# A split-float32 transformer kernel: order of its tensors in the partition

## What is computed

```
m = rms_norm(mem, mem_norm_g)
for layer in (0, 1):
    h = h + mixer(rms_norm(h, mix_norm_g[layer]))
    h = h + memory_cross_attention(rms_norm(h, xa_norm_g[layer]), m, wq, wkv, wo)
    h = h + (gelu(conv3(g) + b) * u) @ w_down,   [u, g] = rms_norm(h) @ w_up
u = rms_norm(h); proj = u @ w_in                  # 9232 columns, second block
h = h + (sigmoid(gate_r) * y_ret + sigmoid(gate_d) * y_dn) @ w_o
h = h + (silu(a) * b) @ w_down,   [a, b] = conv3(rms_norm(h) @ w_up) + b
out = rms_norm(h, g_final)
```

## Time and profile before

| | |
|---|---|
| median of 3 runs | 2487.08 us |
| the profiled execution's own time | 2488.18 us |
| its span, first to last instruction | 2486.4 us |
| TensorE matmuls busy | 2392.3 us, 96% of the span, 10,934 matmuls |
| TensorE weight loads busy | 1926.0 us |
| VectorE, ScalarE, GpSimd busy | 993.0, 865.9, 969.4 us |
| mean granted TensorE clock | 0.99 of full speed |
| read from memory | 213.9 MB, 88 GB/s |

### The profile page before, as it was taken

How to read it: one execution, slowest core, us unless ns; L and a number is a source line. 1 busy time by engine, 2 the same in 40 slices (tenths; PEclk the granted TensorE clock), 3 DMA queues, 4 the chain that set the end, 5 groups by cost and what they waited for, 6 DMA issues and landing times.

```text
span 2486.4 us, 25675 instructions
## 1 busy us (share of the span) xinstructions
PE 2392.3 (96%) x10934; PEld 1926.0 (77%) x10934; DVE 993.0 (40%) x1210; ACT 865.9 (35%) x1048; POOL 969.4 (39%) x389
## 2 busy tenths in 40 slices
PE   8989999999999999999999999988997999999997
PEld 6738878888887887888887768877876888888885
DVE  3053024442244203444226340568458433566601
ACT  4244434322322433433344372351352243322221
POOL 4504713544444561444344314330140144455541
PEclk9999999999999999999999999999999999999998
DMA  7203412333333441323334303420130023333331
GB/s 213 89 0 96 150 43 93 97 99 93 93 97 90 127 128 50 94 93 100 95 98 127 85 26 103 116 77 18 44 93 18 26 93 127 93 100 95 94 95 66
DMA packets 148561, 219.81 MB, mean 88 GB/s; under 512 B 18640, under 2 KB 75216, under 8 KB 148064
## 3 DMA queue, kind: packets, MB, share of 16 engines
q1 hardware_dynamic: 147328, 213.95, 28.5%
q10 hardware_dynamic: 1120, 4.23, 0.5%
HBM read 213.92 MB, written 4.23 MB: 88 GB/s over the span
## 4 chain that ended last, share of the span: by engine, by line
PE 92%; DVE 5%; ACT 2%; issue 1%; DMA 0%; POOL 0%; SPq 0%; ACTq 0%; DVEq 0%
PE ps L916 76%; PE ps L1062 2%; PE ps L1059 2%; PE ps L1280 1%; PE ps L1075 1%; PE ps L1098 1%; PE ps L988 1%; DVE MT L1830 1%; PE ps L1269 1%; PE ps L1168 1%; PE ps L1181 1%; PE ps L1004 1%; PE ps L1221 1%; DVE MM L1834 0%; PE ps L939 0%
## 5 line engine op out<-in xcount | busy, mean ns | idle before, releaser
L474 POOL TENSOR_TENSOR w_lo<-w_raw,w_hi 128x1024 fp32r<-128x1024 f32 x379 | 957.8, 2539 | 1475.8 <-ACT w_hi L511 1475.7
L916 PE MATMUL ps<-XH,w_hi 128*128 128x512 f32 x1792 | 703.0, 392 | 12.7 <-DVE XL L1408 11.9
L511 ACT ACTIVATE w_hi<-w_raw 128x1024 fp32r<-128x1024 f32 x379 | 395.0, 1055 | 887.2 <-DMA w_raw<-ffn_w_up 124.7
L916 PE MATMUL ps<-XH,w_lo 128*128 128x512 f32 x1792 | 698.1, 390 | 0.0
L916 PE MATMUL ps<-XL,w_hi 128*128 128x512 f32 x1792 | 698.1, 390 | 0.0
L916 PE MATMUL ps<-HID,w_hi 128*128 128x512 f32 x1760 | 554.5, 396 | 4.0 <-DVE TY L1613 2.4
L916 PEld LDWEIGHTS ps<-XH,w_hi 128*128 128x128 f32 x1792 | 336.9, 188 | 85.6 <-issue 14.2
L916 PEld LDWEIGHTS ps<-HID,w_hi 128*128 128x128 f32 x1760 | 330.1, 188 | 87.1 <-issue 3.4
L916 PEld LDWEIGHTS ps<-XL,w_hi 128*128 128x128 f32 x1792 | 337.0, 188 | 72.0 <-issue 2.4
L916 PEld LDWEIGHTS ps<-XH,w_lo 128*128 128x128 f32 x1792 | 336.9, 188 | 70.2
L916 PE MATMUL ps<-HID,w_lo 128*128 128x512 f32 x880 | 347.7, 395 | 0.0
(11 more groups left out here) (310 smaller groups left out, 2356.8 us busy)
## 6 DMA issues: line engine op xcount, KB each, us to landing
w_raw<-w_in SPq DMA_DIRECT2D x72, 512.0 KB, 3.7
w_raw<-ffn_w_up SPq DMA_DIRECT2D x128, 256.0 KB, 2.9
w_raw<-w_up SPq DMA_DIRECT2D x88, 256.0 KB, 3.1
w_raw<-xa_wkv SPq DMA_DIRECT2D x32, 512.0 KB, 3.6
w_raw<-ffn_w_down SPq DMA_DIRECT2D x32, 512.0 KB, 3.6
w_raw<-w_in_c SPq DMA_DIRECT2D x24, 512.0 KB, 3.7
w_raw<-w_down SPq DMA_DIRECT2D x22, 512.0 KB, 3.6
w_raw<-w_in_ab SPq DMA_DIRECT2D x16, 512.0 KB, 5.1
```

Of the source, the lines that this page charges most:

```text
L474: nc.gpsimd.tensor_tensor(w_lo[:, s, :, :], w_raw[:, s, :, :], w_hi[:, s, :, :].bitcast(F32), ALU.subtract).then_inc(lo_done, 1)
L511: nc.scalar.activation(w_hi[:, s, :, :], w_raw[:, s, :, :], ACT.Copy).then_inc(hi_done, 1)
L916: mm = nc.tensor.matmul(ps[:, bank + m, :], a, b, start=start and j == 0 and n == 0, stop=stop and j == 1 and n == 2)
```

## The change

The definitions of XH and XL now come first, then the arena with its base a0, then H, the weight rings and the small tensors in their old order. No instruction, size, wait or loop is changed.

```
--- before.py
+++ after.py
@@ -94,9 +94,11 @@
             return ctx.enter_context(nc.semaphore(name))
 
 
-        H = sb("H", [P, KT, T])
         XH = sb("XH", [P, KT, T], F32R)
         XL = sb("XL", [P, KT, T], F32R)
+        a0 = (nc.sbuf_base + 63) // 64 * 64
+        arena = sb("arena", [P, (BIG_SLOTS * T * 4 + TAIL + 64) // 4])
+        H = sb("H", [P, KT, T])
         w_raw = sb("w_raw", [P, RING, 2, UC])
         w_lo = nc.alloc_sbuf_tensor_at("w_lo", [P, RING, 2, UC], F32R, offset=nc.sbuf_base - RING * 2 * UC * 4)
         w_hi = sb("w_hi", [P, RING, 2, UC], F32R)
@@ -110,8 +112,6 @@
         cst = sb("cst", [P, N_CONST, P])
         eps_c = sb("eps_c", [P, 2])
         sm = sb("sm", [P, 128])
-        a0 = (nc.sbuf_base + 63) // 64 * 64
-        arena = sb("arena", [P, (BIG_SLOTS * T * 4 + TAIL + 64) // 4])
         ps = ctx.enter_context(nc.psum_tensor("ps", [P, 8, T], F32))
 
         def at(name, kb, shape, dt=F32):
```

## The result

The changed kernel takes **2522.97 us** (median of 4 runs, 2522.11 to 2525.83); the kernel before, beside it, 2486.71 us (4 runs, 2486.05 to 2490.66). The ratio is 1.0131, 95% interval 1.0119 to 1.0143: slower by 1.3%. The prediction was 2525. The profiled execution took 2522.11 us, against 2488.2 before.

A forecast was written before the change was run, and what follows sets the result against it. It took the kernel to be bound by a stream of TensorE matmuls, number times start-to-start pace. Terms 36.0 + 0 + 1.9 + 0.4 + 0 = +38.3 us on 2487.1 gave 2525 us; range 2471 to 2529.

The forecast's parts named there:

- The main term: XH and XL streaming past loaded weights: 5,400 matmuls go from 226.7 to 233.3 ns, +36.0 us.
- line 1062, a small case: Weights streaming low, MH or ML loaded high: 229.0 and 233.3 ns; taken as the model for XH; itself +0.4 us.
- the 288: Matmuls streaming weights with XH or XL loaded: expected to go to HID's 233.3 ns, +1.9 us.
- the gain that looked due to it: HID streaming, 2,640 matmuls, moved to low addresses: could win 17.6 us at 226.7 ns; taken as 0.
- only the streamed operand's place counts: Rival: HID, now low, speeds up by 17.6 us, XH stays; 2472 to 2474 us, chance 0.22.
- The trace can't tell these two properties apart; each is a place.: Operand lying below or above 92,000 bytes, and start at or 64 past a multiple of 128, treated together; no size.
- Above 233.3 ... none exists either: Rival: split products slower than 233.3 ns, needing high places on both sides, absent after the change; beyond 2529, chance 0.03.
- It becomes what HID is now: high streamed, low loaded: Reason given for matmuls streaming weights past XH or XL to slow to 233.3 ns: +1.9 us.
- Line 1059, "I take 0": 384 matmuls of 256 columns, at 114.5 and 116.4 ns: no change, bounds -0.4 and +0.4 us.
- "Nothing is absorbed": Slower TensorE stretches every stage; its idle time stays the same waits in the same places, so the sum shows fully.
- The faster rival: HID gains from streaming low, XH keeps its pace: 2472 us, or 2474 with HID's upper third above 92,000; chance 0.22.
- The rule of the Trainium skill: Rival for all TensorE matmuls: independent read ports, so addresses change nothing; 2487 us, no effect given chance 0.05.

The follow-up runs named there:

- e8: Kernel before with the weight rings 160 bytes further up and HID starting at 192 modulo 256; 2526.31 us (one run).
- e10: Kernel before with XL alone moved to 192 modulo 256, weights and HID starting alike with XH; 2499.22 us (one run).
- e1: Kernel before with the arena's base rounded up to 128 bytes, so HID, MH and ML lie 64 bytes higher; 2471.82 us, ratio 0.992.
- e2: Changed kernel with the arena 64 bytes longer, so all operands start at multiples of 128; 2518.85 us, ratio to the kernel before 1.0115.

## Why the prediction was right

**The main term.** 5,400 matmuls from 226.7 to 233.3, +36.0 us: found in every stage. What carried it was line 1062, a small case, but the only one in which the loaded operand had the place that the change gives it. By distance it wasn't the case: line 1062 has 64, XH and HID after the change 192. That its slower pace, 233.3, is also that of 192 was luck; the 288, which got line 1062's distance, went to its other pace, 229.0. The prediction also denied HID the gain that looked due to it, with the same row, and so the rival "only the streamed operand's place counts" fell: HID streams from the lower part now and is at 700.

**"The trace can't tell these two properties apart; each is a place."** True, and the right thing to say; what decides is a third that contains neither, the distance modulo 256. The forecast held because the change gave XH the distance that HID has had, 192 (128 less 192; before, 64 less 128), and left HID at 192. The distance could have been read from the rows: XH at 0, HID at 192, line 1062 at 64.

**"Above 233.3 ... none exists either"** was right for this kernel; in e8 one exists, 234.3.

**Small terms that failed.** *"It becomes what HID is now: high streamed, low loaded"*: the 288 went to 229.0, +0.6 us and not +1.9. By distance they have 64 (192 less 128), not HID's 192; places were matched by kind and not by their difference. *Line 1059, "I take 0":* +0.9 us, over the bound of 0.4; its distance stayed 192, so this isn't explained. *"Nothing is absorbed"* failed: 4.0 us net of 37.9 were. The prediction took the clock to be at its full level and left it there; in three short stretches it was lower before the change than after, and the other way round in the delta rule. Span against span the three make 38.3 - 1.3 + 0.9 - 4.0 = 33.9. The medians differ by 36.3, as the profiled execution of before lay 1.5 us above its median and that of after 0.9 below. *The faster rival* was priced at 2474: of the last stage only some 120 matmuls would stream low parts from above 92,000, 0.8 us and not 2.

**The rule of the Trainium skill** (SBUF — State Buffer, "Who interferes with whom", two independent read ports, TensorE waits on nobody) was taken to mean that no address matters, and gave 2487. The runs contradict that for the split products: the distance between what is streamed and what is loaded moves the pace from 226.7 to as much as 234.3. Whether the two ports are independent isn't tested. For plain float32 matmuls the runs agree with it: line 1221 keeps 429 ns at distances of 0, 32, 64, 96, 128 and 192.

**What stays open.** The mechanism inside the memory or the array: no run here has the matmuls without the weight loads beside them, so that it is a collision of the two streams is argued, not shown. Why distances 64 and 128 have two paces each, and how a pair acts on its neighbours, is open too.

## What to carry to other kernels

Where TensorE streams without gaps, read its pace from first and last start of one tile, stage by stage; two paces for one form on one line point at the operands' addresses. For matmuls of this type and 512 columns, let streamed and loaded operands start the same number of bytes past a multiple of 256: here that takes 64 bytes in the kernel before (2471.8 us) or 192 in the changed one (2470.7 us), and either is faster than both kernels of this change (0.992 of the kernel before). And an order of allocations is never changed by itself: look what the rounding of every start behind it becomes. For a difference of a few us, look at the granted clock stage by stage as well: here eight matmuls at half clock cost 1.6 us.

## What the runs showed that wasn't expected

- The addresses of two operands modulo 256 bytes move a kernel bound by TensorE by 2.2% (2470.7 to 2526.3), with no instruction changed.
- Sixteen bytes are enough: 226.7 to 231.7 ns.
- Pairs that alternate between two distances cost more than a count of them gives: 696 ns a triple in e10, where 682.4 was due.
- With 256 columns (line 1059) it is the other way round: at distance 0 in e1 a matmul takes 22.0 / 61 = 361 ns a triple, some 120 each, at 192 before 114.5 to 116.4 and after 22.61 / 192 = 117.8. Aligning all costs this line 384 x 4.5 = 1.7 us, against the 17.6 that HID gains. At 192 alone it has three paces, and in one layer of e2, at 128, it has 120 as well; so here the distance decides less clearly.
- Short stretches at half clock come and go from kernel to kernel: 0.59 and 1.00 for the same matmuls at 801 us before and at 813 us after.
